# A hybrid decoder trunk with eight experts on one core: the small routing operations of VectorE gathered in one block behind the first expert's eighth weight quantum

## What is computed

```python
def _moe(x, router, wg, wu, wd):
    logits = (x @ router).astype(jnp.float32)
    top_val, top_idx = lax.top_k(logits, TOP_K)          # TOP_K = 2
    top_w = jax.nn.softmax(top_val, axis=-1)
    gate = jnp.sum(jax.nn.one_hot(top_idx, N_EXPERTS, dtype=jnp.float32) * top_w[..., None], axis=-2)
    y = jnp.zeros_like(x)
    for e in range(N_EXPERTS):                           # N_EXPERTS = 8
        y = y + gate[..., e:e + 1].astype(x.dtype) * _swiglu(x, wg[e], wu[e], wd[e])
    return y
```

## Time and profile before

| | us |
|---|---|
| median of 3 runs | 1393.92 (1393.74 to 1393.98) |
| the profiled execution | 1392.64 |
| its span, first to last instruction | 1390.4 |
| PE busy in the span | 1366.6 (98%) |
| DVE busy | 1138.7 (82%) |
| ACT busy | 1007.4 (72%) |
| POOL busy | 32.4 (2%) |

### The profile page before, as it was taken

How to read it: one execution, slowest core, us unless ns; L and a number is a source line. 1 busy time by engine, 2 the same in 40 slices (tenths; PEclk the granted TensorE clock), 3 DMA queues, 4 the chain that set the end, 5 groups by cost and what they waited for, 6 DMA issues and landing times.

```text
span 1390.4 us, 19292 instructions
## 1 busy us (share of the span) xinstructions
PE 1366.6 (98%) x6882; PEld 1141.3 (82%) x6882; DVE 1138.7 (82%) x1196; ACT 1007.4 (72%) x1185; POOL 32.4 (2%) x37
## 2 busy tenths in 40 slices
PE   8999999999999999999999999999999999999997
PEld 7779989988787888888888888888888888888886
DVE  5675655556569999999999999999999989999997
ACT  5665544457548778778877877887787788778776
POOL 1201000000001000000000000000000000000010
PEclk9999999999999999999999999999999999999999
DMA  9457754353479999999999999999999999999970
GB/s 330 164 205 279 288 182 156 131 191 133 168 273 370 393 386 355 396 372 364 379 384 371 364 389 375 362 382 381 371 357 394 373 365 382 379 365 374 385 273 32
DMA packets 180620, 436.95 MB, mean 314 GB/s; under 512 B 4070, under 2 KB 8332, under 8 KB 180572
## 3 DMA queue, kind: packets, MB, share of 16 engines
q1 hardware_dynamic: 176816, 422.74, 82.2%
q0 software_dynamic: 3680, 13.54, 2.6%
q10 hardware_dynamic: 76, 0.02, 0.0%
HBM read 423.18 MB, written 13.11 MB: 314 GB/s over the span
## 4 chain that ended last, share of the span: by engine, by line
PE 92%; DVE 4%; ACT 3%; DMA 0%; issue 0%; SPq 0%; DVEq 0%; ACTq 0%
PE ps L1545 26%; PE ps L1546 26%; PE ps L1547 26%; PE ps L1800 3%; PE ps L1802 3%; PE ps L1801 3%; PE ps L2069 2%; DVE w_lo L933 1%; ACT w_hi L540 1%; DMA ring_a<-in_w_in_even 0%; PE ps L1572 0%; PE ps L2040 0%; ACT e L595 0%; DVE xt_lo L972 0%; DVE w_lo L1427 0%
## 5 line engine op out<-in xcount | busy, mean ns | idle before, releaser
L1427 DVE TENSOR_TENSOR w_lo<-ring_a,w_hi 128x1024 fp32r<-128x1024 f32 x384 | 460.0, 1223 | 40.4 <-ACT w_hi L816 30.8
L816 ACT ACTIVATE w_hi<-ring_a 128x1024 fp32r<-128x1024 f32 x384 | 399.7, 1058 | 70.7 <-PE ps L1547 70.6
L1427 DVE TENSOR_TENSOR w_lo<-ring_b,w_hi 128x1024 fp32r<-128x1024 f32 x288 | 345.5, 1223 | 27.5 <-ACT w_hi L816 24.3
L1545 PE MATMUL ps<-w_hi,xg_hi 128*128 128x512 f32 x896 | 356.4, 398 | 2.1 <-DVE w_lo L1427 1.1
L1546 PE MATMUL ps<-w_lo,xg_hi 128*128 128x512 f32 x896 | 353.1, 394 | 0.0
L1547 PE MATMUL ps<-w_hi,xg_lo 128*128 128x512 f32 x896 | 351.5, 392 | 0.0
L816 ACT ACTIVATE w_hi<-ring_b 128x1024 fp32r<-128x1024 f32 x288 | 300.7, 1058 | 55.2 <-PE ps L1547 55.2
L933 DVE TENSOR_TENSOR w_lo<-ring_a,w_hi 128x1024 fp32r<-128x1024 f32 (+2 forms) x119 | 141.7, 1198 | 116.0 <-ACT w_hi L540 115.9
L540 ACT ACTIVATE w_hi<-ring_a 128x1024 fp32r<-128x1024 f32 (+2 forms) x119 | 121.8, 1032 | 130.3 <-PE ps L1802 65.2
L1545 PEld LDWEIGHTS ps<-w_hi,xg_hi 128*128 128x128 f32 x896 | 168.4, 188 | 41.7 <-DVE w_lo L1427 3.1
L1547 PEld LDWEIGHTS ps<-w_hi,xg_lo 128*128 128x128 f32 x896 | 168.3, 188 | 37.9
(11 more groups left out here) (321 smaller groups left out, 1342.1 us busy)
## 6 DMA issues: line engine op xcount, KB each, us to landing
ring_a<-in_moe_wg SPq DMA_DIRECT2D x40, 2048.0 KB, 9.6
ring_a<-in_moe_wu SPq DMA_DIRECT2D x32, 2048.0 KB, 10.0
ring_b<-in_moe_wd SPq DMA_DIRECT2D x32, 2048.0 KB, 9.5
ring_b<-in_moe_wu SPq DMA_DIRECT2D x24, 2048.0 KB, 9.8
ring_a<-in_moe_wd SPq DMA_DIRECT2D x24, 2048.0 KB, 9.1
ring_b<-in_moe_wg SPq DMA_DIRECT2D x16, 2048.0 KB, 10.4
ring_a<-in_ffn_wg SPq DMA_DIRECT2D x5, 2048.0 KB, 8.7
ring_a<-in_ffn_wu SPq DMA_DIRECT2D x5, 2048.0 KB, 7.8
```

The source lines that it names most:

```text
L816: nc.scalar.activation(w_hi[:, (Q1 + q) % NQ, 0:1024], slot(j % RING2)[:, 1024 * k:1024 * k + 1024], ACT.Copy).then_inc(hi_done, 1)
L1427: v.tensor_tensor(w_lo[:, (Q1 + q) % NQ, 0:1024], slot(j % RING2)[:, 1024 * k:1024 * k + 1024], w_hi[:, (Q1 + q) % NQ, 0:1024].bitcast(F32 ...
L1545: pe.matmul(out_, a_hi, w_hi[:, q, c0:c1], start=first, stop=False)
```

## The change

In the VectorE program the order around the start of expert 0 is written anew. Before, `gates()` stood between the rest of quantum 2 and `xg_lo`; `extras()` and `token_rows()` between the rest of quantum 3 and that of quantum 4; `kept_gates()` behind that of quantum 7. Now `xg_lo` follows the rest of quantum 2, the rests of quanta 3 to 7 follow at once, and all four routines follow those, ahead of the loop, whose first work is the rest of quantum 8. No instruction is added or removed, and no other engine's program changes.

```diff
             choose(0)
             for q in range(NQ - 1):
                 expert_rest(0, q)
+            gathered_rests(0)
+            for q in range(NQ - 1, AHEAD):
+                expert_rest(0, q)
             gates()
-            gathered_rests(0)
-            expert_rest(0, NQ - 1)
             extras()
             token_rows()
-            for q in range(NQ, AHEAD):
-                expert_rest(0, q)
             kept_gates()
             with dve.Fori(0, NE - 1) as i:
                 item_rests(i, AHEAD, False)
```

## The result

| | before | after |
|---|---|---|
| median, us (6 runs each) | 1393.88 | 1399.18 |
| range of the runs | 1392.46 to 1394.34 | 1398.08 to 1399.93 |
| the profiled execution | 1392.64 | 1399.93 |
| its span | 1390.4 | 1397.8 |

The ratio is 1.0039, with a 95% interval of 1.0029 to 1.0049: 4.0 to 6.8 us slower. Measured a second time, among the experiments, it gave 1.0048 (1.0034 to 1.0062).

The account below looks back on a forecast made before the run. PE's work plus its holes was taken as the bound; quantum 8 starting 4.46 us late plus 2.0 for the clock gave 1393.92 + 6.46 = 1400.4 us, with 8 in 10 between 1397.7 and 1401.9.

Parts of the forecast that it names:

- the start of expert 0: DVE ahead of xg_lo: taking gates() away only lets DVE wait for ACT's xg_hi; gain taken as 0.
- Quanta 4 to 7: Expert 0: their rests come earlier, PE runs them without a hole, 1.36 us gained for the moment.
- The block: The 46 small instructions on DVE, now ahead of the rest of quantum 8: 7.98 us, from 421.00 to 428.98.
- the sum: PE starts quantum 8 at 430.26 instead of 425.80, 4.46 us later, and nothing behind it makes this up.
- The clock: PE idle 6.0 us ahead of quantum 8: if its clock falls, 2.0 us more, bounds 0.6 and 2.9; otherwise 0.
- The likelier case: The clock falls inside PE's hole ahead of quantum 8: chance 0.62, between 1398.9 and 1401.3, likeliest 1400.4 us.
- The rule on short VectorE operations: 58 + FD cycles for SBUF operations would make the block 3.7 us, no change; the profile's 0.16 us row was preferred.
- The profile and the median: Whole kernel: the profiled execution should come to 1399.1 us and the median to 1400.4, a shift of 6.46.
- The clock stays up: Rival: PE's clock does not fall in the hole ahead of quantum 8; 1398.4 us, chance 0.28.
- Hidden block: Rival: the block fits into PE's cover behind quantum 7; not slower, 1392.2 at full gain; hidden or nearly, chance 0.05.
- Weights held up: Rival: late scatters hold SP's weight loads until ACT waits, some 5 us more, 1405; with dearer low-clock stretch, chance 0.05.

Follow-up runs that it names:

- gates_back: Changed kernel with gates() alone put back ahead of xg_lo, the other three routines staying behind quantum 7; median 1398.37 us, ratio 1.0035 to the kernel before.
- filled_one: Changed kernel with one extra unused 256-column matmul on PE ahead of quantum 8 of expert 0; median 1399.71 us, ratio 1.0048 to the kernel before.
- rows_back: Changed kernel with gates(), extras() and token_rows() between the rests of quanta 3 and 4, kept_gates() behind quantum 7; median 1396.07 us, ratio 1.0023.
- after, again: The changed kernel run once more without edit, beside the kernel before on the same chip; median 1399.87 us, ratio 1.0048.
- filled: Changed kernel with ten extra unused 256-column matmuls on PE in the hole ahead of quantum 8; median 1397.93 us, ratio 1.0033 to the kernel before.
- spread: Changed kernel with gates() in its old place, extras() between rests 3 and 4, token_rows() and kept_gates() behind quantum 7's; median 1392.94 us, ratio 0.9997.
- best: Against the kernel before: small tiles in pad_rows, extras() split, gates() and kept_gates() moved into expert 7; median 1391.74 us, ratio 0.9988.

## Why the prediction was right

*What bounds the kernel, and the start of expert 0.* Right: `xg_lo` did not move against the work ahead of it, and gates_back showed from the other side that `gates()` costs nothing in DVE's wait.

*Quanta 4 to 7.* Right: no hole of PE at quantum 4.

*The block, and the sum.* Forecast 7.98 us from 421.0 to 429.0, measured 7.99 from 420.85 to 428.84. Forecast shift of quantum 8 4.46 us, measured 4.49. Nothing was made up behind it.

*The clock.* The likelier case came. The price was taken as 2.0 us with bounds of 0.6 and 2.9. The traces had 2.2, 2.8, 2.2 (gates_back), 2.3 (filled_one: twelve steps in 5.17 us instead of 2.87) and 1.6 (rows_back), all within the bounds. That the 2.0 came so near is in part luck: it was read from the pace of small matmuls at the program's start, where the granted clock reads 1.00. My reading of where the fall comes was weaker than its outcome. I took the 4.5 us of the program's end for about the length that a hole needs, and the clock fell 4.0, 5.2 (after, again), 2.3 and 3.8 us behind PE's last work in holes of 4.3 to 6.0 us, and 3.4 us behind it with a hole of 2.85. A single row gave one draw of something that varies from one execution to the next.

*The rule on short VectorE operations.* By the row `58 + FD` of the Trainium skill (VectorE: DVE Perf Modes, the errata section) the prediction estimated a block of 3.7 us and no change. The block took 7.99. The same section says that this row gives too short a time and that the measured fixed term is about 150 cycles; by an estimate from it a 2-column operation takes (150 + 2) / 0.96 = 158 ns, and the trace agrees with its 0.16 us. The prediction did not use that sentence.

*The profile and the median.* The profiled execution was forecast at 1399.1 and took 1399.93, of which 0.7 is the output's DMA. The median came out at 1399.18, 1.2 below the forecast of 1400.4, the repeat at 1399.87. The shift of 6.5 stands against 5.3 and 6.5 in the medians and 6.8 and 7.3 in the traces. The low-clock stretch differs from one execution to the next: it cost 2.2 us in one trace of the changed kernel and 2.8 in the other. Whether that makes up the 1.2 us between the two medians' shifts is not shown.

*The rivals.* The clock stays up: 1398.4 was forecast for it, and filled, which keeps it up, has 1397.93 beside a kernel before that is 0.6 lower. Hidden block: refuted by its length. Weights held up: the scatters were as late as forecast (428.37, forecast 428.5), and no weight load came late for ACT.

*What the prediction had not seen.* It added up holes and cover and got the right number, but the shorter account is the one that the experiments bear out. Ahead of quantum 8 DVE has a fixed amount of work and in the kernel before it never waits there. So the rest of quantum 8 comes at the same time in the order in which DVE does not wait (spread, where quantum 8 is +0.01), and later by DVE's waits in the others. Quantum 8 was 4.49 us later against waits of 4.47 in the changed kernel, and 2.74 against 2.72 in gates_back. In rows_back it was quantum 4 on PE that was 1.74 later against 1.72, and the rest of quantum 8 on DVE, 1.75; PE came to quantum 8 later still, by the clock. The prediction named only the first of these waits, the 1.72 ahead of `xg_lo`. The hole of 1.1 us at quantum 4, which the profile shows as PE's longest wait in this part, was worth nothing as long as DVE's work stayed.

## What to carry to other kernels

Where an engine that feeds the bound is itself full over a stretch, count its idle time there, not the holes of the engine that it feeds. As long as the fed engine waits for it at the end of the stretch, an order that lets it wait is slower by just that wait, and one that only moves the hole changes nothing. Small work belongs into the waits that the feeding engine has anyway, or out of the stretch; memory that ties it to the stretch may be worth giving. And price a hole of the matmul engine by more than its length: holes of 2.85 to 6.0 us cost 1.6 to 2.8 us more by the clock here, and ten extra matmuls in the hole gave back 2.2 us in the trace.

## What the runs showed of the hardware

In the traces the granted clock of TensorE fell from 2.4 to 1.2 GHz with every hole between 2.85 and 6.0 us that was left open, and with none of 1.6 or 1.7 us. It fell between 2.3 and 5.2 us behind the last matmul, in rows_back only after work had begun again, and it rose again 4 to 6 us after work had begun (rows_back 4.0, after 4.9, after again 6.1). The Trainium skill (TensorE: Matmul & The Clock Gate, Part 1) states that the clock drops to half after idleness and that activity releases it, and these rows agree. The mean clocks of the executions without a trace suggest, but do not show, that the hole of 2.85 us does not always bring the fall (rows_back, 1394.80 and 1394.92 us at 0.998).

At the low level a 512-column matmul stepped by 0.427 us, at the high one by 0.231. At the high clock the first matmul behind an idle PE took its successor 0.33 us later instead of 0.23. The same 0.33 stands in best at the start of quantum 8, without a hole (428.62 to 428.95), so the idleness is not shown to be its cause.
